# Latent attention: keeping the values in the array and moving scaled probabilities

## The reference

```python
sc = q @ k.T * 96 ** -0.5                 # 512 x 512; q, k normed and rotated, 96 wide
mask = key_chunk[None, :] <= q_chunk[:, None]   # chunks of 64 rows
p = softmax(where(mask, sc, -inf), axis=-1)
o = p @ v                                 # 512 x 64
# o of the 16 heads side by side is 512 x 1024; it is multiplied by w_o
```

## Time and profile before

| what | value |
|---|---|
| median of three runs | 1928.76 us |
| profiled execution, its span | 1928.52 us, 1926.7 us |
| TensorE busy over the span | 1912.5 us, 99% |
| VectorE, ScalarE busy | 63%, 49% |
| granted TensorE clock | 1.00 in all stretches of this stage |
| attention stage, scores of head 0 to the last values of head 14 | 866.6 to 993.1 us |
| VectorE's and ScalarE's busy time in the steps from 10 on, 952.7 to 993.0 us | 30.9 us and 32.4 us of 40.3 us |

### The profile page before, as it was taken

The page is one execution under the profiler, slowest core; times in us unless marked ns, Lnnn a source line. Parts: engine busy times, 40 slices in busy tenths (PEclk is TensorE's granted clock), DMA queues, the critical chain, the costliest instruction groups (busy, mean ns, idle before and its releaser), DMA issues.

```text
span 1926.7 us, 23396 instructions
## 1 busy us (share of the span) xinstructions
PE 1912.5 (99%) x9546; PEld 1624.5 (84%) x9546; DVE 1215.8 (63%) x1653; ACT 940.2 (49%) x1332; POOL 49.9 (3%) x85
## 2 busy tenths in 40 slices
PE   8999999999999999999999999999999999999999
PEld 6889998888888888898888888888888889888887
DVE  5645553345767676876745868667644357776867
ACT  5333334234645445568754644545565546453543
POOL 1000000000000000010000000000000000000000
PEclk9999999999999999999999999999999999999999
DMA  7233322322341431321013142241232223414141
GB/s 250 76 98 96 92 68 97 110 99 88 108 136 41 153 110 65 103 59 46 23 45 127 49 153 83 92 153 44 89 110 66 88 66 110 142 55 153 36 140 69
DMA packets 163398, 182.47 MB, mean 95 GB/s; under 512 B 7682, under 2 KB 125015, under 8 KB 163163
## 3 DMA queue, kind: packets, MB, share of 16 engines
q1 hardware_dynamic: 160746, 176.67, 28.6%
q0 software_dynamic: 2528, 4.29, 0.8%
q10 hardware_dynamic: 16, 0.00, 0.0%
HBM read 175.62 MB, written 2.11 MB: 92 GB/s over the span
## 4 chain that ended last, share of the span: by engine, by line
PE 96%; DVE 2%; ACT 1%; DMA 0%; issue 0%; SPq 0%; ACTq 0%
PE psum L96 29%; PE psum L98 29%; PE psum L97 29%; PE psum L2274 2%; PE psum L2252 2%; PE psum L2706 1%; PE psum L2262 1%; DVE weights_lo L414 1%; PE psum L578 1%; PE psum L2230 1%; PE psum L2694 0%; PE psum L1025 0%; PE psum L1017 0%; PE psum L996 0%; PE psum L1006 0%; PE psum L994 0%
## 5 line engine op out<-in xcount | busy, mean ns | idle before, releaser
L96 PE MATMUL psum<-norm_T_hi,weights_hi 128*128 128x512 f32 (+1 forms) x1440 | 538.2, 374 | 0.2 <-DVE weights_lo L414 0.2
L98 PE MATMUL psum<-norm_T_hi,weights_lo 128*128 128x512 f32 (+1 forms) x1440 | 533.7, 371 | 0.0
L97 PE MATMUL psum<-norm_T_lo,weights_hi 128*128 128x512 f32 (+1 forms) x1440 | 533.3, 370 | 0.0
L414 DVE TENSOR_TENSOR weights_lo<-raw_weights,weights_hi 128x2048 fp32r<-128x2048 f32 (+3 forms) x136 | 299.1, 2199 | 240.6 <-ACT weights_hi L408 240.4
L408 ACT ACTIVATE weights_hi<-raw_weights 128x2048 fp32r<-128x2048 f32 (+3 forms) x136 | 249.4, 1834 | 189.3 <-PE psum L98 189.3
L98 PEld LDWEIGHTS psum<-norm_T_hi,weights_lo 128*128 128x128 f32 x1440 | 271.2, 188 | 46.8
L96 PEld LDWEIGHTS psum<-norm_T_hi,weights_hi 128*128 128x128 f32 x1440 | 271.3, 188 | 45.9 <-DVE weights_lo L414 0.5
L97 PEld LDWEIGHTS psum<-norm_T_lo,weights_hi 128*128 128x128 f32 x1440 | 271.4, 188 | 45.2
L96 PE MATMUL psum<-weights_hi,act_T_hi 128*128 128x512 f32 (+1 forms) x528 | 204.0, 386 | 0.0
L98 PE MATMUL psum<-weights_hi,act_T_lo 128*128 128x512 f32 (+1 forms) x528 | 203.0, 384 | 0.0
L97 PE MATMUL psum<-weights_lo,act_T_hi 128*128 128x512 f32 (+1 forms) x528 | 202.9, 384 | 0.0
(11 more groups left out here) (317 smaller groups left out, 2458.2 us busy)
## 6 DMA issues: line engine op xcount, KB each, us to landing
raw_weights<-in_ffn_w_dram SPq DMA_DIRECT2D x32, 1024.0 KB, 5.6
scratch<-in_ffn_w_dram SPq DMA_DIRECT2D x32, 1024.0 KB, 5.4
raw_weights<-in_w_in_dram SPq DMA_DIRECT2D x26, 512.0 KB, 5.3
raw_weights<-in_w_in_dram SPq DMA_DIRECT2D x11, 1024.0 KB, 5.3
raw_weights<-in_w_up_dram SPq DMA_DIRECT2D x8, 1024.0 KB, 6.9
scratch<-in_w_up_dram SPq DMA_DIRECT2D x8, 1024.0 KB, 6.8
raw_weights<-in_w_down_dram SPq DMA_DIRECT2D x8, 1024.0 KB, 5.4
scratch<-in_w_down_dram SPq DMA_DIRECT2D x8, 1024.0 KB, 5.2
```

The source lines that it names most:

```text
L96: pe.matmul(out, ah, bh, start=start, stop=False, skip_group_check=more)
L97: pe.matmul(out, ah, bl, start=False, stop=False, skip_group_check=more)
L98: return pe.matmul(out, al, bh, start=False, stop=stop, skip_group_check=more)
L414: dve.tensor_tensor(WL[:, u % 2, 0:c], raw(units[u].slot)[:, 0:c], WH[:, u % 2, 0:c].bitcast(F32), SUB).then_inc(w_lo, 1)
```

## The change

`values` now handles a pair of heads. The values stand (64 columns) and the transposed probabilities move; the result comes out transposed, head 2i in output rows 0 to 63 and head 2i+1 in rows 64 to 127 of one bank, and the products of the two heads alternate. So the transpose of the outputs and the column of ones are gone. The denominators come from the exponentials (`accum_out`), and VectorE scales the probabilities before they are transposed (`scaled`, in place of `normed`). PT exists twice, once for each head of a pair, and is laid out by key tile. The values of pairs 0 to 3 come in steps 1, 3, 5 and 7 behind the first two projections, those of pairs 4 to 6 in steps 10, 12 and 14 behind the next head's scores, those of pair 7 in the tail. The emptying of projected values waits for the products that still read the buffer.

```diff
-            PT = SCR[:, 0:NTRI * P]
+            PT = [SCR[:, c:c + 2048].rearrange("p (j t q) -> p j t q", j=NT, t=NT) for c in (0, 13728)]
...
                 def turn(n, c):
-                    pe.wait_ge(pex.sem, pex.at(4 * n + RAISED[c]))
+                    pe.wait_ge(psc.sem, psc.at(4 * n + RAISED[c]))
...
-                def values(n):
-                    if n:
-                        pe.wait_ge(ond.sem, ond.at(n))
-                    for t in ORDER:
...
-                        for j in range(t + 1):
-                            mm = pe.matmul(PS[:, 6, t * MV1:t * MV1 + MV1], PT[:, off[t] + j * P:off[t] + j * P + P],
-                                           VN[:, n // 4 % 2, j, n % 4, :], start=j == 0, stop=j == t)
+                def values(pair):
+
+                    n = 2 * pair + 1
+                    pe.wait_ge(pte.sem, pte.at(2 * n + 2))
+                    pe.wait_ge(a1.sem, a1.at(n + 1))
+                    if pair:
+                        pe.wait_ge(paired.sem, paired.at(pair))
+                        pe.wait_ge(tl.sem, tl.at(pair))
+                    for j in range(NT):
+                        t = max(j, 1)
+                        for b in range(2):
+                            h = n - 1 + b
+                            pe.matmul(PS[b * MV:b * MV + MV, OUT, t * P:S], VN[:, h // 4 % 2, j, h % 4, :], PT[b][:, j, t:NT, :],
+                                      start=j == 0, stop=True, skip_group_check=j > 0)
+                    for b in range(2):
+                        h = n - 1 + b
+                        mm = pe.matmul(PS[b * MV:b * MV + MV, OUT, 0:P], VN[:, h // 4 % 2, 0, h % 4, :], PT[b][:, 3, 2, :],
+                                       start=True, stop=True)
                     mm.then_inc(pvd.sem, 1)
...
                     scores(n + 1)
+                    if n > MH // 2 and n % 2 == 0:
+                        values(n // 2 - 1)
                     turn(n, 0)
...
                     turn(n, 2)
-                    for what in before:
+                    for what in gemms[:2]:
                         job(what)
-                    values(n)
-                    for what in gemms:
+                    if n < MH // 2 and n % 2:
+                        values(n // 2)
+                    for what in gemms[2:]:
                         job(what)
...
-                tail.extend((last_turn, lambda: values(MH - 1), lambda: job(("out", MH // 2 - 1))))
+                tail.extend((last_turn, lambda: values(MH // 2 - 1)))
...
                         act.wait_ge(gemm, gb + 8 * g + 4 + t + 1)
+                        if g > 1:
+                            act.wait_ge(pvd.sem, pvd.at(2 * g - 2))
...
                         act.activation(SB[:, off[t]:off[t] + w], SB[:, off[t]:off[t] + w], ACT.Exp,
-                                       bias=nms[:, n % 2, t:t + 1], scale=qs[:, n // 4 % 2, t, n % 4:n % 4 + 1]).then_inc(pex.sem, 1)
+                                       bias=nms[:, n % 2, t:t + 1], scale=qs[:, n // 4 % 2, t, n % 4:n % 4 + 1],
+                                       accum_out=den[:, n % 2, t:t + 1]).then_inc(pex.sem, 1)
...
-                def normed(n):
-                    dve.wait_ge(pvd.sem, pvd.at(n + 1))
...
+                def scaled(n):
+
+                    for c, ts in enumerate((slice(3, 4), slice(0, 3))):
+                        dve.wait_ge(pex.sem, pex.at(4 * n + (1, 4)[c]))
+                        dve.reciprocal(rden[:, n % 2, ts], den[:, n % 2, ts]).then_inc(rcp.sem, 1)
+                        dve.wait_ge(rcp.sem, rcp.at(2 * n + c + 1))
+                        for t in (ORDER[:1], ORDER[1:])[c]:
+                            z = SB[:, off[t]:off[t] + (t + 1) * P]
+                            dve.tensor_scalar(z, z, rden[:, n % 2, t:t + 1], None, MUL).then_inc(psc.sem, 1)
...
                     if n in SPLITS:
                         split_lo(dve, u0 + SPLITS[n])
-                    normed(n)
+                    if n + 1 < MH:
+                        scaled(n + 1)
```

More of the change, by code:

```diff
@@ L2181, in mla @@
                     order += slot
-            order.append(("out", MH // 2 - 1))
             idx = {job: m for m, job in enumerate(order)}
@@ L2210, in job @@
                         pe.wait_ge(ev.sem, ev.at(emptied[last]))
-                        if order[last][0] == "out":
-                            pe.wait_ge(tl.sem, tl.at(order[last][1] + 1))
                     kind = what[0]
@@ L2230, in job @@
                             mm = pe.transpose(PS[0:MQK, bank(m), t * P:t * P + P], QK[:, h // 4 % 2, j, t, h % 4, :], IDENT[:, :])
-                        mm.then_inc(tp.sem, 1)
-                    else:
-                        pe.wait_ge(ond.sem, ond.at(2 * what[1] + 2))
-                        for t in range(NT):
-                            mm = pe.transpose(PS[:, bank(m), t * P:t * P + P], ON[:, t, :], IDENT[:, :])
                         mm.then_inc(tp.sem, 1)
@@ L2283, in _ @@
                 for n in range(MH):
-                    behind, between, before, gemms = jobs_at(n)
+                    behind, between, gemms = jobs_at(n)
                     if n + 1 == MH:
@@ L2387, in _ @@
                         split_hi(act, u0 + SPLITS[n])
+                    if n % 2 == 0 and n:
+                        pair_hi(n // 2 - 1)
                     for c in (0, 2):
@@ L2406, in _ @@
                         squares(g + 1, 0)
-                empty(("out", MH // 2 - 1))
+                pair_hi(MH // 2 - 1)
             @block.gpsimd
@@ L2518, in _ @@
                 masks(0)
+                scaled(0)
                 for n in range(MH):
@@ L2560, in freed @@
                     pe.wait_ge(masked.sem, masked.at(4 * MH))
-                elif j == 0:
-                    pe.wait_ge(made.sem, made.at(MH // 2 - 1))
-            return tail, lambda pe, k: pe.wait_ge(made.sem, made.at(k + 1)), freed, (bank(len(order) - 2), bank(len(order) - 1))
+            return tail, lambda pe, k: pe.wait_ge(made.sem, made.at(k + 1)), freed, OUT
         def mlstm(block, norm, came, banks):
@@ L2974, in build @@
             compressed = mla_down(block, after, came, dn, up)
-            tail, made, freed, (spare, taken) = mla(block, compressed, dn)
-            banks = ((0, 1, 2, spare), (3, 4, 6, taken))
+            tail, made, freed, taken = mla(block, compressed, dn)
+            banks = ((0, 1, 2, 5), (3, 4, 7, taken))
             up, dn, turn = bank_sets(banks)
```

76 lines of the change are left out of this document (33 added, 43 removed).

## The result

| kernel | median us | range, executions |
|---|---|---|
| before | 1928.62 | 1928.19 to 1929.55, 9 |
| after | 1935.59 | 1932.75 to 1940.67, 9 |

The change makes the kernel slower: ratio 1.0034, 95% interval 1.0025 to 1.0042, that is 7 us. The forecast was 1931.3 us, in 1925 to 1945, with slower as the likeliest side. The nine executions of after are not alike, though. Each comes with the mean granted clock of TensorE, where 1.000 means its upper level (2.4 GHz) all the time: two at 1.000 took 1932.75 and 1932.78 us, six at 0.998 took 1934.95 to 1936.01, and one at 0.995 took 1940.67. Before is at 1.000 in every execution for which the clock is on record. So there are two things to explain: 4.1 us at the upper clock, and 2 to 3 us more in most executions.

The account below looks back on a forecast made before the run. TensorE, busy 99% of the span, was taken to bound the kernel. Waits of 21.3 us against 18.4 us saved made it 2.9 us slower (2.8 with rounding), from 1928.52 to 1931.3 us, range 1925 to 1945.

Parts of the forecast that it names:

- The saving: Values on TensorE: a pair of heads takes 2.5 us instead of 4.80, eight pairs save 18.4 us.
- Rival B2: Pair's products overlap, but one half's weight loads wait for the other's product: 3.5 us a pair, 1938.5 us; chance 0.11.
- (a): Scores wait for ScalarE's key copy after steps 0, 4 and 8 to 13, 1.19 us each: 9.5 us.
- (e): Step 9: `norm` and `rotate` push head 10's mask and head 12's keys, delaying scores: 0.9 us.
- (b): Late scaling of chunk 0 on VectorE in steps 0, 4, 8 and 10 keeps TensorE waiting: 5.6 us.
- Rival C: Masks and scalings run ahead, so no chunk is late: 8.2 us less, 1923 us; chance 0.12.
- (c): First head: nothing hides its probabilities' scaling, so turns 0 and 1 wait 0.8 us more each: 1.6 us.
- (d): Steps 3 and 7: the third kv projection waits for a bank whose copies wait for the pair's values: 1.8 us.
- (f): Steps 3 and 5, banks and table loads behind the turns, 0.9 us; step 13, weight split and chunk 1 scaling, 1.0.
- The freed wait of the output projection costs nothing.: Start of the output projection: freeing its wait was listed among the edits that cost nothing.
- I expect the granted clock to stay at its upper level.: TensorE's waits are well under a microsecond or two each, so its clock stays at 2.4 GHz.
- rival B: The two heads' products don't overlap at all: 4.3 us a pair, 15.9 us slower, 1944.4 us; chance 0.22.

Follow-up runs that it names:

- the variant without the remedy: The kernel with five edits, less the edit that puts the pair ahead of the key and value projections in steps 3, 7 and 11: 1929.04 us.
- the experiment: After, with each of the output projection's first three groups waiting only for the mask that empties its own bank: 1933.72 us.
- the first filling: After, plus eight idle transposes of the identity where TensorE waits for the key copy (steps 0, 4, 8 to 13): 1934.65 us.
- five edits: After, with finer projection wait, pairs ending odd steps, even-step key copy first, pairs before key/value projections (steps 3, 7), weight splits in steps 7 and 15: 1927.47 us.

## Why the prediction was right

**The saving, forecast 18.4 us.** The step was right, and its mechanism nearly. A pair's products take 2.31 us, not 2.5: both heads together need 7 per cent more than one head alone in the serial order (2.15 us), so there are no five slots, but almost full overlap. But the change of the array's shape, costed at nothing by the earlier trace rows, is not free. The scores take 2.16 us from start to start behind a projection and 2.26 us behind a pair (2.21 behind the values of before); and the first product of a pair starts 0.27 us after the last product of a projection, where two such products are 0.17 apart:

```profile
885.06 0.33 PE L97 MATMUL psum<-weights_lo,act_T_hi 128*128 128x384 f32 x1
885.23 0.34 PE L98 MATMUL psum<-weights_hi,act_T_lo 128*128 128x384 f32 x1
885.50 2.16 PE L2270 MATMUL psum<-scratch 128*64 128x384 f32 x16
...
887.81 2.43 PE L2245 MATMUL psum<-key_rows,plain_act 96*128 96x512 f32 x8
890.07 0.60 PE L2255 MATMUL psum<-ident,scratch 128*128 128x128 f32 x4
...
895.18 2.32 PE L2245 MATMUL psum<-key_rows,plain_act 96*128 96x512 f32 x8
897.34 0.60 PE L2255 MATMUL psum<-ident,scratch 128*128 128x128 f32 x4
```

With up to 0.1 us at either end a pair costs 2.5 us, and eight save 18.4. The sum was right by luck, two errors of 0.2 us that cancel. The Trainium skill (TensorEngine Tiling (Array Packing), Key Properties) has a change of the tiling mode drain TensorE; the trace agrees with some cost, 0.1 us a change, less than the 0.16 us that I had worked out by the rule. Another rule of the Trainium skill that I weighed (TensorE: Matmul & The Clock Gate, Part 3, The mechanism), that a weight load overlaps a running product only if the row group differs, does not hold here: both heads use all 128 rows, and the pair's loads start two by two every 0.32 us (979.00, 979.32, 979.64 us) while TensorE's products run without a gap. Rival B2 falls with it.

**(a) The key waits, forecast 8 x 1.19 = 9.5 us.** There are seven, before the scores of heads 2, 6, 10 and 12 to 15; before those of head 11 the masks come last, so that the eighth wait lies inside (e). Each costs 1.04 + 0.16 = 1.20 us, 8.4 us in all. Right in place and size.

**(b) Late scaling, forecast 5.6 us.** The rows before the turns of heads 1, 5, 9 and 11 are 0.58, 1.00, 1.00 and 1.33, with 0.16 each 4.5 us. Right in place, 1.1 us too large: each forecast was 0.1 to 0.5 us long. For step 0 the terms as I gave them make 4.1 - 3.35 = 0.75 us, not the 1.0 that I put in the sum; measured is 0.74. For step 10 they make +5.1, not +5.5, so 1.7 us; measured is 1.49. The durations themselves came as worked out from the earlier trace rows, and the exponential with its read moves the next by 0.80 us for 512 columns. The groups by form of after:

```profile
L2355 ACT ACTIVATION_READ_ACCUMULATOR scratch<-scratch,small 128x1 f32 x64 | 12.2, 190 | 0.0
...
L2489 DVE TENSOR_SCALAR scratch<-scratch,small 128x512 f32<-128x512 f32 x16 | 7.8, 486 | 0.6
L2489 DVE TENSOR_SCALAR scratch<-scratch,small 128x384 f32<-128x384 f32 x16 | 6.7, 420 | 0.6
L2489 DVE TENSOR_SCALAR scratch<-scratch,small 128x256 f32<-128x256 f32 x16 | 5.6, 348 | 0.0
...
L2489 DVE TENSOR_SCALAR scratch<-scratch,small 128x128 f32<-128x128 f32 x16 | 4.5, 281 | 0.0
```

0.49, 0.42, 0.35 and 0.28 us against 0.48, 0.42, 0.35 and 0.28. The kernel without the scaling shows that what it costs as a whole is 5 us, not the 7.4 us of the rows for the scaling and the masks, since ScalarE is late next. Rival C is refuted by these waits.

**(c) First head, forecast 1.6.** From its scores to the end of its turns before takes 6.94 us, after 875.80 - 867.29 = 8.51: 1.6 us. **(d) forecast 1.8:** two waits of 0.82, with 0.16 each 2.0 us, and the variant without the remedy is 1.6 us slower than the one with it. **(e) forecast 0.9:** before the scores of head 11 TensorE now waits 1.51 and 0.30 us for masks, with 0.16 each 2.1 us, and the key wait that I counted in (a) is inside it; less the 0.6 us of before that is 1.5 us. **(f) forecast 1.9:** four waits for ScalarE's copies, 2.1 us with their ends, less 1.2 of before: 0.9 us. Two more parts leave no idle row on PE. In steps 1, 3 and 5 the first product of a projection needs the bank that ScalarE's copy of the queries empties; only its weight load shows the wait:

```profile
882.15 0.19 PEld L96 LDWEIGHTS psum<-weights_hi,act_T_hi 128*128 128x128 f32 x1 [0.19 <-ACT plain_act L2330]
...
900.23 0.19 PEld L96 LDWEIGHTS psum<-weights_hi,act_T_hi 128*128 128x128 f32 x1 [0.31 <-ACT plain_act L2330]
...
920.65 0.19 PEld L96 LDWEIGHTS psum<-weights_hi,act_T_hi 128*128 128x128 f32 x1 [0.30 <-ACT plain_act L2330]
```

From the start of the two transposes ahead to that product are 0.33, 0.48 and 0.47 us, where steps 2 and 6 have 0.14: 0.9 us in all. And the scaling of head 13's chunk 1 holds TensorE for 0.3 us in step 13 (987.58 - 986.86 = 0.72 us for four transposes, 0.44 otherwise). With these (f) is 2.0 us, near its forecast.

**"The freed wait of the output projection costs nothing."** This is the step that failed. The values of head 14 used to stand between the last scores' masks and the projection. I had taken them out and costed the wait at nothing, without asking what hides it now. It is 1.59 + 0.16 = 1.75 us, and the experiment gets 1.2 to 2.0 us back.

**The sum.** At the upper clock: 8.4 + 4.5 + 1.6 + 2.0 + 1.5 + 2.0 + 1.75 = 21.8 us of waits; against 18.4 saved, 3.4 us slower. Measured is 4.1 us (1932.77 against 1928.62), and the stage of the first filling's profile, which adds only transposes inside waits and ran at 1.00, is 130.67 us long, 4.2 us above before. So some 0.7 us are in none of these terms. They may be that work behind a wait starts slowly: four transposes take 0.49 us from start to start there, 0.44 otherwise, and scores 2.26 instead of 2.16 to 2.21; over some 20 waits that is up to 1 us by estimate from these rows. It was not measured by itself.

**"I expect the granted clock to stay at its upper level."** This failed too, and it is worth 2 to 3 us of the 7. The reason that I gave, waits well under a microsecond or two each, is what the rows refute: in after every wait in the stage is 1.6 us at most, and the clock falls nonetheless where several of them come close together. The profiled execution shows what a fall costs. From scores to scores the step of head 15 has its scores in 3.14 us and its pair in 3.15, where the first filling has 2.36 and 2.31. Part of the first fall is given back: of 0.74 + 0.90 us lost on the scores of head 11 and the pair behind them only 0.7 are left when head 15 begins, since the wait for the scaling of head 11 in between is 1.33 us there and 1.65 in the first filling, which also waits 0.45 us for a copy of queries in that step.

So the range and the side were right. 2.8 us slower was 4.1 at the clock that I assumed, and the clock made it 7. The range was set wide for rival B; the likeliest case's own range, 1927 to 1936, holds the measured 1935.6 only just.

## What to carry to other kernels

Work taken from TensorE is a gain only where no copy, mask or scaling becomes due in the place that it leaves: here 18 us were saved, and 22 us of waits of 0.2 to 1.6 us each took their place. Before work is removed, list for each place what would end last there without it, every wait at the edge of the stage too. And the order has then to be made anew: five small edits took back 8 us, most of it by putting the remaining work where the waits are; but what an engine does late may be late because another engine's queue needs what stands ahead of it.

## What the hardware showed

Products that use different halves of the array's columns and different halves of the output rows run at the same time in float32, with all 128 rows in use, if they alternate in program order: 2.31 us against 4.08 us in series. Each change between full-width and half-width products cost up to 0.1 us.

TensorE's clock fell to its lower level where idle times of 0.3 to 1.5 us came close together; idle transposes in these steps kept it up in 10 of 11 executions. One fall cost from nothing to be seen (five edits) to 2 us (first filling), and whether it comes differs from execution to execution of one kernel, so the time of after spreads over 7.9 us where that of before has 1.4 us.
